# Two-layer diffusion backbone on one core: layers written out, the four expert groups gathered at once and run as one sequence of 32 experts

## What is computed

```python
def hier_moe(h, w_coarse, w_fine, w1, w3, w2):
    x = h.reshape(b * l, d)
    p_coarse = jax.nn.softmax((x @ w_coarse).astype(jnp.float32), -1)
    p_g, g_sel = lax.top_k(p_coarse, 1)
    ...
    top_v, top_i = lax.top_k(fine_g, MOE_TOP_K)
    ...
    hid = jax.nn.silu(jnp.einsum('td,edf->tef', x, w1)) * jnp.einsum('td,edf->tef', x, w3)
    y = jnp.einsum('tef,efd->td', hid * gates[:, :, None], w2)
    ...
# in each layer:
    xp = layer_norm(DEEPNORM_ALPHA * xp + g1 * out, ln_g[l, 0], ln_b[l, 0])
    ff = hier_moe(xp * (1 + sc2) + sh2, ...)
    xp = layer_norm(DEEPNORM_ALPHA * xp + g2 * ff, ln_g[l, 1], ln_b[l, 1])
```

## Time and profile before

| | |
|---|---|
| median of 3 runs | 1664.62 us (1659.61 to 1665.06) |
| span of the profiled execution | 1651.8 us |
| TensorE busy, weight loads | 1458.4 us (88%), 1083.8 us (66%) |
| VectorE, ScalarE busy | 1020.7 us (62%), 750.5 us (45%) |
| moved by DMA | 345.20 MB, mean 209 GB/s |
| mean granted TensorE clock | 0.932 of full speed |

### The profile page before, as it was taken

One profiled execution on the slowest core, in us unless ns is written; L12 is line 12 of the kernel. 1 busy time (PEld: TensorE's weight loads), 2 busy tenths in 40 slices (PEclk: granted clock), 3 DMA queues, 4 the chain that ended last, 5 costly groups with the idle time before them and its releaser, 6 DMA issues.

```text
span 1651.8 us, 20067 instructions
## 1 busy us (share of the span) xinstructions
PE 1458.4 (88%) x6572; PEld 1083.8 (66%) x6572; DVE 1020.7 (62%) x1137; ACT 750.5 (45%) x702; POOL 28.9 (2%) x44
## 2 busy tenths in 40 slices
PE   5989999998699898989799899999878989999893
PEld 0227877877577676767512587878757777777672
DVE  0026667657668686868620456666666876868685
ACT  0023454543267465656300444636214655656470
POOL 3000000000000000000010000000000000000000
PEclk9999999998789898999889999999796999999897
DMA  9875434323169595969588653433232886969580
GB/s 316 278 265 176 145 115 147 128 103 127 56 219 349 206 349 203 348 242 340 188 263 295 215 167 116 165 109 128 81 128 68 317 303 251 332 227 349 202 316 27
DMA packets 101681, 345.20 MB, mean 209 GB/s; under 512 B 8436, under 2 KB 11856, under 8 KB 91856
## 3 DMA queue, kind: packets, MB, share of 16 engines
q1 hardware_dynamic: 98544, 332.87, 57.3%
q0 software_dynamic: 3040, 11.15, 2.3%
HBM read 341.35 MB, written 3.67 MB: 209 GB/s over the span
## 4 chain that ended last, share of the span: by engine, by line
PE 41%; DVE 34%; DMA 7%; ACT 7%; issue 5%; DVEq 4%; ACTq 1%; SPq 0%
PE bank L703 39%; DVE wl L1434 22%; DMA raw<-in_moe_w 5%; ACT wh L1373 3%; PE bank L706 3%; DMA raw<-in_w_ada 2%; DVE hid L1965 1%; DVE hTTl L1434 1%; ACT wh L1187 1%; DVE tmp L1434 1%; DVE x L1434 1%; DVE merged L1434 1%; DVE xgl L1938 1%; DVE x L1536 0%; DVEq L1925 0%
## 5 line engine op out<-in xcount | busy, mean ns | idle before, releaser
L1434 DVE TENSOR_TENSOR wl<-raw,wh 128x2048 fp32r<-128x2048 f32 (+1 forms) x268 | 610.5, 2278 | 226.2 <-ACT wh L1187 161.3
L1373 ACT ACTIVATE wh<-raw 128x2048 fp32r<-128x2048 f32 x192 | 367.4, 1915 | 65.1 <-PE bank L703 36.8
L703 PE MATMUL bank<-wh,xgh 128*128 128x512 f32 x512 | 212.7, 415 | 14.1 <-DVEq L1939 11.5
L703 PE MATMUL bank<-wh,hTh 128*128 128x512 f32 (+2 forms) x512 | 204.3, 399 | 16.0 <-DVEq L1506 16.0
L703 PE MATMUL bank<-wh,xgl 128*128 128x512 f32 x512 | 204.8, 400 | 0.0
L703 PE MATMUL bank<-wl,xgh 128*128 128x512 f32 x512 | 204.0, 399 | 0.0
L703 PE MATMUL bank<-wh,hTl 128*128 128x512 f32 (+2 forms) x512 | 199.1, 389 | 0.0
L703 PE MATMUL bank<-raw,cT 128*2 128x512 f32 x384 | 174.7, 615 | 27.0 <-DMA raw<-in_w_ada 22.6
L1187 ACT ACTIVATE wh<-raw 128x2048 fp32r<-128x2048 f32 (+2 forms) x78 | 142.4, 1833 | 111.8 <-PE bank L703 83.3
L703 PE MATMUL bank<-wl,hTh 128*128 128x512 f32 (+1 forms) x480 | 187.3, 390 | 0.0
L703 PEld LDWEIGHTS bank<-raw,cT 128*2 128x2 f32 x384 | 32.4, 87 | 160.0 <-issue 134.2
(11 more groups left out here) (252 smaller groups left out, 1687.7 us busy)
## 6 DMA issues: line engine op xcount, KB each, us to landing
raw<-in_moe_w SPq DMA_DIRECT2D x256, 512.0 KB, 5.0
raw<-in_moe_w SPq DMA_DIRECT2D x64, 1024.0 KB, 6.9
raw<-in_w_in SPq DMA_DIRECT2D x52, 1024.0 KB, 5.0
raw<-in_w_ada SPq DMA_DIRECT2D x48, 1024.0 KB, 5.3
raw<-in_w_branch SPq DMA_DIRECT2D x12, 1024.0 KB, 5.5
raw<-in_w_o SPq DMA_DIRECT2D x8, 1024.0 KB, 4.9
lnrow<-in_ln_rows POOLq DMA_DIRECT2D x4, 1024.0 KB, 4.9
raw<-in_w_in SPq DMA_DIRECT2D x4, 544.0 KB, 4.0
```

The source lines that it names most:

```text
L703: return behind(nc.tensor.matmul(*args, **kw))
L1373: tally(A_(wh[c][:, :], raw[:, r, :], ACT.Copy), part_high[c])
L1434: return V.tensor_tensor(o, a, b, op)
```

## The change

- Both layers are written out, without `Fori`: all counts and addresses are constants. `rounds` is split: `more_rounds` (wait for `need`, `value_load`) stands ahead of the first round on PE, ACT, DVE and behind it on SP, `second_round` (the `If`) behind it.
- One gather for all four groups: DVE writes `selg` for all groups (8 instructions), TensorE makes 16 results of 512 columns (2 matmuls each) in six banks, ACT and DVE copy 8 each.
- 32 experts as one sequence (`EXPERTS`), with two banks for `up`. TensorE's order is up(q, first half), turn_hidden(q-1), up(q, second half), down(q-1). ACT and DVE convert piece 3q+2 ahead of `sil` and `hid` of q, and 3q+3, 3q+4 behind them. The first two pieces are converted ahead of the router's results.
- The groups' sums are kept split in `ygh`, `ygl` (four each, in the place of `xgh`, `xgl`), and all scatters stand at the end, around down(31). The matmuls with zeros fall away.
- The rows of gate 2 are made at experts 8, 10, 12, 14: 4 matmuls and an ACT copy each, to `gate2`. The residual (`moe_residual`) reads them from there.

```diff
-        def rounds(eng, waited, l, one_round, before_skip):
-
-            eng.sem_inc(waited, 1)
-            one_round(Tally(eng), 0)
+        def more_rounds(eng, waited, l):
+
             eng.wait_ge(need_ready, l + 1)
             eng.sem_inc(waited, 1)
-            more = eng.value_load(need[0:1, 0:1], min_val=0, max_val=1)
+            return eng.value_load(need[0:1, 0:1], min_val=0, max_val=1)
+
+        def second_round(eng, more, one_round, before_skip):
+
             tally = Tally(eng)
             with eng.If(more > 0):
                 one_round(tally, 1)
...
-                    up(0)
-                    turn_hidden(0)
-                    for e in range(1, EPG):
-                        up(e)
-                        down(e - 1)
-                        turn_hidden(e)
-                    if prepare:
-                        gather(tally, rnd, g + 1, 0)
-                    down(EPG - 1)
...
+                def gather(tally, rnd):
+
+                    pe.wait_ge(sel_ready, N_R.moe(l, rnd, 1))
+                    for c in range(DC):
+                        for part, src in (("h", x2h), ("l", x2l)):
+                            name = f"xg{part}{c}"
+                            t = round_free(pe, l, rnd, name)
+                            for s in range(2):
+                                ins = mm(t[:, :], src[:, s, c * P:(c + 1) * P], selg[:, s, :], start=s == 0, stop=s == 1)
+                            tally(ins, full[IN_ROUND[name][0]])
...
+                    for q in range(E):
+                        if q == 0:
+                            pe.wait_ge(xg_act, N_X.moe(l, rnd, 4))
+                            pe.wait_ge(xg_dve, N_X.moe(l, rnd, 4))
+                        up(q, 0)
+                        if q == 0:
+                            slot_gates(tally, rnd)
+                            pe.wait_ge(xg_act, N_X.moe(l, rnd, DC))
+                            pe.wait_ge(xg_dve, N_X.moe(l, rnd, DC))
+                        else:
+                            turn_hidden(q - 1)
+                        up(q, 1)
+                        if q:
+                            down(q - 1)
+                        if q == 1:
+                            turn_selection(tally, rnd)
+                        if q in GATE2_AT:
+                            gate2_rows(tally, rnd, *GATE2_AT[q][0:2])
+                    scatter(0)
+                    turn_hidden(E - 1)
+                    scatter(1)
+                    down(E - 1)
+                    scatter(2)
+                    scatter(3)
...
+                    for q in range(E):
+                        if q:
+                            turned_hidden(tally, rnd, q - 1)
+                        if q > 1 and (q - 1) % EPG == 0:
+                            take_sums(tally, rnd, (q - 2) // EPG)
+                        if q == 0:
+                            t = round_full(dve, l, rnd, "gg")
+                            tally(V.tensor_copy(gg[:, :], t[:, 0:E]), free[IN_ROUND["gg"][0]])
+                            drain()
+                        convert(tally, rnd, 3 * q + 2 if q else 3)
+                        dve.wait_ge(sil_done, N_E.moe(l, rnd, q + 1))
+                        b = UP_BANKS[q % 2]
+                        tally(V.scalar_tensor_tensor(out=hid[:, :], in0=bank[b][:, FF:2 * FF], scalar=gg[:, q:q + 1],
+                                                     in1=sil[:, :], op0=ALU.mult, op1=ALU.mult), free[b])
+                        tally(drain(), hid_ready)
+                        for j in (3 * q + 3, 3 * q + 4) if q else (4,):
+                            if j < len(EXPERTS):
+                                convert(tally, rnd, j)
```

More of the change, by code:

```diff
@@ L85 @@
 SPLIT = PIECES[RAW:]
[L87 to L91, removed]
+EXPERTS = [("up", 0, 0), ("up", 0, 1)]
+for _e in range(1, E):
+    EXPERTS += [("up", _e, 0), ("up", _e, 1), ("down", _e - 1)]
+EXPERTS += [("down", E - 1)]
+assert MOE0 % SLOTS == 0 and len(EXPERTS) % SLOTS == 0 and len(SPLIT) % PARTS == 0 and len(EXPERTS) % PARTS == 0
 ROUNDS = 2
@@ L378, in hybrid_backbone @@
             ("cbm", [P, 2, 2, P], F32, 10),
-            ("lnrow", [P, 2, D], F32, 0))
-        bias, kctx, vctx, xs, seg = region(
+            ("lnrow", [P, 2, D], F32, 0),
+            ("hTTh", [P, 2, P], F32R, 8), ("hTTl", [P, 2, P], F32R, 9),
+            ("sil", [P, FF], F32, 10), ("hid", [P, FF], F32, 11))
+        bias, kctx, vctx, xs, seg, selg, selT = region(
             "context", 8,
@@ L585, in _ @@
             sp.dma_start(cs[:, 1, :], A["c"][0].rearrange("(p c) -> p c", c=DC)).then_inc(once, 16)
-            with sp.Fori(0, L) as l:
+            for l in range(L):
                 for i, piece in enumerate(PIECES):
@@ L643, in _ @@
             pool.wait_ge(bias_laid, 16 * 4 * L)
-            with pool.Fori(0, L) as l:
+            for l in range(L):
                 pool.wait_ge(ln_used, 2 * l + 1)
@@ L826, in _ @@
             pe.wait_ge(c_ready, 1)
-            with pe.Fori(0, L) as l:
+            for l in range(L):
                 def turn_small():
@@ L1176, in _ @@
             A_(tmp[:, 0:16].rearrange("p (s c) -> p s c", s=2), cs[:, :, :], ACT.Silu).then_inc(c_exp, 1)
-            with act.Fori(0, L) as l:
+            for l in range(L):
                 def convert_to(i):
@@ new lines, in take_sums @@
+                def take_sums(tally, rnd, g):
+                    for n in range(2):
+                        t = bank[SUM_BANKS[n]]
+                        act.wait_ge(full[SUM_BANKS[n]], N_BANK[SUM_BANKS[n]].moe(l, rnd, IN_ROUND[f"sum{g}{n}"][1] + 1))
+                        tally(A_(ygh[g][:, n * 512:(n + 1) * 512], t[:, :], ACT.Copy), yg_high)
+                more = more_rounds(act, act_waited, l)
+                one_round(Tally(act), 0)
+                second_round(act, more, one_round, act.drain)
@@ L1471, in layer_norm @@
                         done.then_inc(ready, 1)
-            with dve.Fori(0, L) as l:
+            for l in range(L):
                 def convert_to(i):
```

532 lines of the change are left out of this document (273 added, 259 removed).

## The result

The changed kernel takes 1549.05 us (median of 5 runs, 1542.22 to 1552.37) against 1664.62 for the kernel before (1659.61 to 1665.63): a ratio of 0.932, 95% interval 0.929 to 0.935. On another chip it was 1545.01 against 1659.22, 0.931 (0.928 to 0.933). The forecast was 1553.

A forecast was written before the change was run, and what follows sets the result against it. No one engine bounds the whole; group borders empty the engines, and without them transfers narrowly bound the experts. Layer sums of -55.9 and -55.8 make -111.7, taking 1664.6 to 1553 us, own range 1540 to 1568.

The forecast's parts named there:

- mixers: Token mixers: only waits on counts in registers go, -2 us a layer, between 0 and -12.
- start of the stage: Router to first `hid`: selections, value load and the one gather make it +3.5 us a layer, 0 to +12.
- 31 distances: First to last `hid` of a layer: at 9.05 us each, 280.6 us, so -47.9 and -50.6.
- end of the stage: Last `hid` to last scatter: three scatters around down(31), turn and waits, 9.4 us for 7.88, +1.5 a layer.
- between the layers: Last scatter to `w_ada`: gate rows and loop's end go, `w_ada` loads start earlier; -11 us, -15 to -8.
- end of the kernel: Last scatter to VectorE's first product: only VectorE's jump of 3.5 us remains of 11.65; -8.2, -7 to -10.
- The period: Time per expert without group borders, the largest of four floors: transfers narrowly bound it, 9.05 us, between 8.7 and 9.4.
- Rival (a): Expert stages: transfers keep up with the compute floors, 8.7 us per expert, 22 less, 1531 us; chance 0.22.
- The gate rows: Mid-stage: their ACT copies fit its 2 us slack per expert; otherwise about 1 us each, four times.
- (c): Expert stages: a late piece ahead of `sil` and `hid` puts all in series, 11.4 us per expert, 1699 us; chance 0.04.
- (d): Group borders only let loads recover, so each expert takes 10.7 us, 1655 us or more; chance 0.02.
- sign of being wrong: Mid-stage: `hid` over 9.5 us apart, ACT waiting for loads each expert, or TensorE at the lower clock.

The follow-up runs named there:

- experiment 3: Changed kernel with SP adding the skipped round's slot counts and VectorE waiting for the scatter banks behind its jump; 1546.00 us, ratio 0.930.
- 10: Changed kernel with other PSUM banks for the next layer's first outputs; 1550.87 us, ratio 0.935.
- 11: Changed kernel with other banks, SP adding the skipped round's slot counts and VectorE's bank wait behind its jump; 1541.92 us, ratio 0.928.
- Experiment 1: Kernel before with only its two layers written out, loops over groups and order of work kept; 1630.22 us, ratio 0.979.
- the second profile: The changed kernel itself, unaltered, run and profiled again on another chip; 1545.01 us, ratio 0.931 to the kernel before.
- 2: Kernel before with its layers and the loop over the four groups written out, same order of work; 1622.78 us, ratio 0.977.

## Why the prediction was right, and where it was not

The time came out 4 us under the forecast, inside its own range. In the spans the sum is met to 0.3 us; the 4 us are that the profile after lies 8.7 us below its median and the profile before 12.8 below, which the forecast carried over. That the sum is met so closely is luck: the terms are off by 14 us one way and 13 the other. Against the span, in us:

| term | predicted | measured, layer 0 / 1 |
|---|---|---|
| mixers | -2 each | -0.2 / -2.7 |
| start of the stage | +3.5 each | +2.9 / +2.3 |
| 31 distances | -47.9 / -50.6 | -52.3 / -53.6 |
| end of the stage | +1.5 each | +3.3 / +3.2 |
| between the layers | -11 | -4.7 |
| end of the kernel | -8.2 | -6.4 |
| ahead of the first mixer, output | 0 | -3.5, +0.4 |
| sum | -111.7 | -111.4 |

*The period.* Predicted 9.05 (8.95 to 9.2), "the transfers become the bound, narrowly"; measured 8.91 and 8.95 on average, at the lower edge. Wrong was the step from "the four slots now never rest" to a bound: the commonest distance is TensorE's 8.63, and with a sixth of the bytes gone the stage hardly moved. VectorE's floor was right (8.5, measured 8.47). TensorE's came out right (8.7, measured 8.63) by two errors that cancel: the 36 matmuls take 8.40 and not 8.2, and the turn takes 0.23 for its two matmuls and not for each, because the 3.67 for 16 of the earlier trace rows stand ahead of the matmuls spaced 0.427, at the lower clock. The transfers' floor was put too high, up to 9.28. Rival (a) named the mechanism, T = 8.7. Why is the mean then 8.91? In layer 0: 31 times 8.63 is 267.5; the first distance is 7.29 (-1.3), the turn of the selections +0.8, the three distances with sums +5.0 (one of them with a gate row), the three other gate rows +2.2. That makes 274.2. The 1.9 that are left are, as far as shown, what late loads cost: the stretches in which ACT hardly waits for loads are 273.9 (experiment 3) and 273.7 and 274.6 (half of `w2`).

*The gate rows.* That their copies lie in ACT's "2 us of slack per expert" looked at the wrong engine. Eight matmuls of 0.11 are on TensorE, which is the bound: 9.31 for 8.40 in the chain, 0.91 a row. That the stage gets shorter without them is not shown (-1.3 and +0.5 against the mean of 276.2).

*End of the stage.* Mis-sized, 1.5 for 3.3. At the last `hid` TensorE, now the bound, still has the end of down(30) and scatter(0), 1.8, which the sum left out; from 748.05 to 759.23 it has no idle time.

*Between the layers.* The step that failed is that SP "starts about when the last piece is converted". The piece was converted at 747.92, SP issued at 762.88: the counts of the skipped round are added behind VectorE's jump. A second thing was not seen at all, the bank 4 that the last scatter holds until 768.13. Experiments 3, 10 and 11 show that each alone hides the other. With both gone the seam is 8.7 us under that before. TensorE then comes 5.9 us behind the scatter: the jump is the 4.0 of the forecast (by luck: it is that long with the early loads beside it, and 1.7 behind the scatter without them, 759.23 to 760.90), and the counts behind it, 1.5, were left out of the sum. The wait for a load in mid-stage was kept, as forecast (3.93 us at 799.51).

*End of the kernel.* VectorE's jump with its counts was put at 3.5; the first product comes 5.3 us behind the scatter. VectorE's idle time is 7.28 and 7.54, where the forecast leaned on TensorE's 4.35 and 4.50. At the seam, where the same path could be split, the jump was 2.8 and the counts 1.9. With the wait behind the jump the product comes 2.3 behind the scatter, without a jump 0.3.

*The start.* The gather took 9.7 us (454.26 to 463.95), as computed, partly at the lower clock; the value load shows as 1.11 us of idle, but taking it out does not shorten the stretch.

*The mixers.* What writing out the layers gives was forecast as 2 a layer and lies within what two profiles of one kernel differ by. Experiment 1 showed more than its own expectation, because it took register waits out of the expert loop too; the prediction had those in its period.

*Ahead of the first mixer.* The -3.5 is within chance: the second profile has 123.26, 1.7 more than before.

Rivals (c) and (d) did not occur: in the profile after no distance is over 10.9, and the clock in mid-stage is 1.00. One sign of being wrong came near: ACT waits for loads 21 times in the 31 distances of layer 0, 16.4 us in all. It cost some 2 us a layer, as said.

## What to carry to other kernels

When floors lie within a few per cent, forecast the period by the highest engine floor plus what is inserted into that engine, and treat a transfer share of 0.94 as nearly but not yet the bound; then relief of one floor alone is worth 1 to 2%. Ask of every moved step which engine it uses, not which engine waits for it. Where two waits end together, as the bank and the first load at the seam, remove both or neither: one alone measured 0. Counts that only say "this was skipped" should be added by whoever waits for them, ahead of the jump (0.09 us each on VectorE here), and a wait of the main path stands better behind such a jump than ahead of it (5.3 to 2.3 us at the kernel's end). And check at which clock level a row was taken before using it as a price.

## What the runs showed beside it

- A jump is dearer while weights are being loaded. Over the second round VectorE's takes 2.7 to 3.5 us without loads and 5.07 and 5.69 us with the `w_ada` loads under way, in the same kernels that have 2.74 and 3.04 at their end. The page lists packets of a kind "instruction" among the DMA queues (55 and 40 in the changed kernel), so instructions that come late through busy transfer engines would explain it; no run shows that this is the way.
- The skipped second round, a jump and some counts on four engines, costs with the seam's bank 18 us of 1545: by the profiles 15 at the seam, 5 at the end. Some 2 to 3 of them are the clock after TensorE's idle time.
- At the first group border the granted clock was 0.85, 0.95 and 1.00 in three kernels whose engines do the same work there, with borders of 24.28, 21.54 and 19.55 us. The clock is not all of the difference, and what made it fall is open.
- The expert matmuls of 512 columns are spaced 0.233 us in the changed kernel and 0.228 in the kernel before and in experiments 1 and 2 (means over 540 to 690 pairs between 560 and 745 us), whether the transfers run at a share of 0.84 or 0.94, with half of `wl` left out and with one bank for `up` too. In the mixers it is 0.232 and 0.233. For 36 matmuls it is 0.18 us, 5 us a layer. No run tells its cause.
